# Two down projections with 25 paired steps of seven products instead of 12 paired steps in one of them

## The reference

```python
def conv_ffn(h, w_up, conv_w, conv_b, w_down):
    u = causal_depthwise_conv(h @ w_up, conv_w, conv_b)
    val, gate = jnp.split(u, 2, axis=-1)
    return (jax.nn.gelu(gate) * val) @ w_down      # (256 x 5632) @ (5632 x 2048)
...
for layer in range(DEPTH):                          # DEPTH = 2
    ...
    x = x + conv_ffn(rms_norm(x, ffn_norm[layer]), ...)
```

## Time and profile before

| | us |
|---|---|
| median of three runs | 2266.3 (2266.22 to 2268.31) |
| the profiled execution | 2266.04 |
| its span, first to last instruction | 2264.4 |
| PE busy | 2254.7 |
| DVE busy | 1559.0 |
| ACT busy | 1289.7 |
| POOL busy | 642.8 |
| down0, first to last matmul of layer 0's down projection, about | 967.5 to 1206.8 |
| down1, the same of layer 1's, about | 2028.3 to 2260.8 |

### The profile page before, as it was taken

How to read it: one execution, slowest core, us unless ns; L and a number is a source line. 1 busy time by engine, 2 the same in 40 slices (tenths; PEclk the granted TensorE clock), 3 DMA queues, 4 the chain that set the end, 5 groups by cost and what they waited for, 6 DMA issues and landing times.

```text
span 2264.4 us, 33777 instructions
## 1 busy us (share of the span) xinstructions
PE 2254.7 (100%) x11036; PEld 1902.6 (84%) x11036; DVE 1559.0 (69%) x1892; ACT 1289.7 (57%) x1692; POOL 642.8 (28%) x1051
## 2 busy tenths in 40 slices
PE   9999999999999999999999999999999999999999
PEld 7888888988888888888888888898888888888887
DVE  6766775676767667665556678758767667678666
ACT  6655664565556555554444777556656556555444
POOL 1720001234343343412221000215344343432100
PEclk9999999999999999999999999999999999999999
DMA  8656335546676776766665555646876676778876
GB/s 277 207 197 205 134 123 177 177 152 220 217 224 210 225 218 215 223 208 201 202 204 186 186 186 169 203 140 204 250 223 214 220 222 214 221 226 237 271 225 198
DMA packets 150694, 464.70 MB, mean 205 GB/s; under 512 B 26656, under 2 KB 27552, under 8 KB 150608
## 3 DMA queue, kind: packets, MB, share of 16 engines
q1 hardware_dynamic: 121152, 423.55, 57.1%
q0 software_dynamic: 29312, 39.95, 6.5%
q10 hardware_dynamic: 144, 0.06, 0.0%
HBM read 433.17 MB, written 2.10 MB: 192 GB/s over the span
## 4 chain that ended last, share of the span: by engine, by line
PE 96%; DVE 2%; ACT 1%; issue 1%; DMA 1%; POOL 0%; SPq 0%; ACTq 0%; DVEq 0%
PE ps L475 47%; PE ps L480 23%; PE ps L433 10%; PE ps L437 5%; PE ps L418 2%; PE ps L454 2%; PE ps L1003 2%; PE ps L1005 1%; PE ps L816 1%; PE ps L1108 1%; PE ps L802 0%; DVE w_lo L407 0%; PE ps L896 0%; POOL u_t L2343 0%; DMA u_t<-z_t 0%
## 5 line engine op out<-in xcount | busy, mean ns | idle before, releaser
L379 DVE TENSOR_TENSOR w_lo<-raw,w_hi 128x1024 fp32r<-128x1024 f32 x704 | 875.8, 1247 | 585.2 <-ACT w_hi L373 582.6
L373 ACT ACTIVATE w_hi<-raw 128x1024 fp32r<-128x1024 f32 x703 | 741.6, 1059 | 719.3 <-PE ps L480 599.0
L475 PE MATMUL ps<-w_hi,xg_hl 128*128 128x512 f32 (+1 forms) x3392 | 832.1, 387 | 2.1 <-DVE xg_hl L1604 2.1
L475 PEld LDWEIGHTS ps<-w_hi,xg_hl 128*128 128x128 f32 x3392 | 631.3, 188 | 131.3 <-DVE xg_hl L1604 2.0
L480 PE MATMUL ps<-w_lo,xg_hl 128*128 128x512 f32 (+1 forms) x1696 | 449.4, 387 | 0.0
L480 PEld LDWEIGHTS ps<-w_lo,xg_hl 128*128 128x128 f32 x1696 | 316.4, 188 | 65.3 <-DVE w_lo L379 0.4
L475 PE MATMUL ps<-w_hi,a_hl 128*128 128x512 f32 x1464 | 364.5, 391 | 0.3 <-ACT kmem_tok L1240 0.2
L2343 POOL DMA_DIRECT2D u_t<-z_t x704 | 347.6, 502 | 2.8 <-issue 2.8
L475 PEld LDWEIGHTS ps<-w_hi,a_hl 128*128 128x128 f32 x1464 | 272.8, 188 | 57.5 <-issue 0.7
L480 PE MATMUL ps<-w_lo,a_hl 128*128 128x512 f32 x732 | 195.8, 389 | 0.0
L433 PE MATMUL ps<-xg_hl,w_hi 128*128 128x512 f32 x512 | 161.7, 397 | 0.0
(11 more groups left out here) (247 smaller groups left out, 2101.1 us busy)
## 6 DMA issues: line engine op xcount, KB each, us to landing
raw<-in_w_stream SPq DMA_DIRECT2D x775, 512.0 KB, 4.1
u_t<-z_t POOLq DMA_DIRECT2D x704, 34.0 KB, 3.4
t_in<-in_w_stream SPq DMA_DIRECT2D x24, 256.0 KB, 3.4
t_in<-in_w_stream POOLq DMA_DIRECT2D x24, 256.0 KB, 7.5
raw<-in_w_stream SPq DMA_DIRECT2D x14, 256.0 KB, 4.9
bias<-in_rel_bias POOLq DMA_DIRECT2D x4, 768.0 KB, 6.2
memT<-in_mem_t POOLq DMA_DIRECT2D x4, 512.0 KB, 6.2
gate_w<-in_gate_w POOLq DMA_DIRECT2D x4, 512.0 KB, 3.9
```

The lines of the kernel that those rows point to most:

```text
L373: nc.scalar.activation(w_hi[:, s, :], raw[:, s, :], ACT.Copy).then_inc(hi_done, 1)
L379: nc.vector.tensor_tensor(w_lo[:, s, :], raw[:, s, :], w_hi[:, s, :].bitcast(F), ALU.subtract).then_inc(lo_done, 1)
L475: nc.tensor.matmul(ps[:, bank + tt, 0:n], a[:, k0 + k, tt * P:tt * P + P], w_hi[:, s, k * n:k * n + n], start=start and k == 0 and q == 0, ...
```

## The change

All four pairs of blocks, two in each layer, are now taken with paired steps, and one table, `PAIR_ORDER`, gives their order. In it "a" and "b" are single ordinary units of the first and of the second block of a pair. The numbers of paired steps are 5, 5, 7 and 8 (25), all of the kind "s", for which `ADDING` is 2: two weight sums by DVE, two by adding transfers. (The code also knows a kind "d" with one adding transfer; the table doesn't use it.) In the second pair of layer 0 and in both pairs of layer 1 most steps have one "c" (two units) between them. The activation sums are made in batches at new places (`FORMS_AT`), their splits three and four units later. `t_raw` has one buffer instead of two. In layer 0 DVE, not ACT, puts each block together from the banks (`pair_sums`, `first_block`, `second_block`, `last_parts`), and the last block's two parts are added after the last matmul. The 11 second-block units "b" of layer 0 stand at the end of down0; the turned tiles of three blocks are made ready there.

```diff
-PAIRED = 6
-LAST_ORDER = [...]
-FORMS_AT = [0, 2, 10]
+PAIR_ORDER = \
+    [[("c", u) for u in range(5, 11)] + [x for j in range(4) for x in (("s", j), ("c", 11 + 2 * j), ("c", 12 + 2 * j))]
+     + [("s", 4), ("c", 19), ("c", 20), ("c", 21)],
+     [("a", u) for u in range(5, 16)] + [("c", 16)] + [x for j in range(5) for x in (("s", j), ("c", 17 + j))]
+     + [("b", u) for u in range(5, 16)],
...
+FORMS_AT = [[0, 2, 14], [0, 2, 14, 38]]
...
+        t_raw = [at("t_raw0", XG + size([LAYER_FORMS[0], 4, 2, P]), [UE]), at("t_raw1", ZT, [UE])]
...
+            def down_units(l, c0, c1, steps):
+                for c in range(c0, c1):
+                    old = c - SLOTS
...
+                    sp.wait_ge(lo_done, SPLIT_OF.get(old, old + (EXTRA if l else 0)) + 1)
+                    for n in steps:
+                        if old in (RAW_OF[n], RAW_OF[n] + 1):
+                            sp.wait_ge(wsum_ready, 2 * n + 2)
+                        if c == RAW_OF[n] + 6 and n + 2 in steps:
+                            sums_first(n + 2, l)
...
             def down_section():
-                for n in range(4):
-                    if n < 2:
-                        pe.wait_ge(proj_free, fblock["down0"] + n + 1)
-                    else:
-                        pe.wait_ge(dn_out, TT * (n - 1))
-                    for u in range(TOK_DOWN):
-                        token_unit(...)
+                pe.wait_ge(proj_free, fblock["down0"] + 2)
+                block_pair(0, value_there)
+                block_pair(1, None, lambda tile: pe.wait_ge(dn_out, tile + 1))
...
-            def down_tiles(n):                      # ACT
-                act.wait_ge(pe_unit, first["down0"] + TOK_DOWN * (n + 1))
...
-                for tt in range(TT):
-                    A(y_up[:, tt, :], ps[:, 2 * (n % 2) + tt, :], ACT.Copy).then_inc(dn_out, 1)
...
             def rec_section():                      # DVE
                 c0 = first["rec"]
+                dve.wait_ge(pe_unit, c0)
+                for tt in range(TT):
+                    dve.wait_ge(part_ready, tt + 1)
+                    V.tensor_tensor(y_up[:, tt, :], y_part[:, tt, :], ps[:, 2 + tt, :], ALU.add).then_inc(dn_out, 1)
                 for u in range(U_FULL):
...
+            def down_section():                     # POOL
+                for n in range(2):
+                    added(n)
...
+                move(0)
+                added(PAIRS[0] + 1)
+                move(1)
+                squares(0)
+                for n in range(PAIRS[0] + 2, LAYER_PAIRS[0]):
+                    added(n)
```

More of the change, by code:

```diff
@@ L292, in trunk @@
                         ("rec", N_REC), ("out1", N_OUT), ("xq1", N_XQ), ("xo1", N_XO), ("up1", N_UP), ("down1", N_DOWN)):
[L293 removed]
+            first[name] = c + (EXTRA if name in AFTER else 0)
             assert c % SLOTS == 0
@@ L296, in trunk @@
         N_UNITS = c
[L298 to L304, removed]
-                else:
-                    SPLITS += [("w", c), ("h", c + 1), ("t", n, 0), ("t", n, 1)]
+        GROUPS, SPLIT, RAW_OF, WSUM_SPLIT, SPLIT_OF, SUM_BEFORE, ADDING = [], {}, {}, {}, {}, {}, []
@@ new lines, in trunk @@
+        GROUP_FROM, HALF = [], set()
+        n = 0
+        for g, order in enumerate(PAIR_ORDER):
+            if g % 2 == 0:
+                e = first["down1" if g else "down0"]
+                c = e - (EXTRA if g else 0)
+            GROUP_FROM.append(e)
+            steps = []
+            for kind, u in order:
+                steps.append((kind, u, e, n))
+                parts = [("w", c)] if kind in "ab" else [("w", c), ("w", c + 1)]
+                if kind in "sd":
+                    parts = [("w", c), ("h", c + 1), ("t", n, 0), ("t", n, 1)]
@@ new lines, in trunk @@
+                c += 1 if kind in "ab" else 2
+                e += len(parts)
+            GROUPS.append(steps)
+            if g == 1:
+                assert e == first["rec"]
+        assert c == N_UNITS
+        END = e
+        PAIR_END = GROUP_FROM[1]
+        STEP0 = [sum(PAIRS[:g]) for g in range(len(PAIRS))]
+        LAST_STEP = [STEP0[g] + PAIRS[g] - 1 for g in range(len(PAIRS))]
+        LAST_SPLIT = [WSUM_SPLIT[n, 1] for n in LAST_STEP]
+        FIRST_OF = [[[u for kind, u, _, _ in steps if kind in ("c", "ab"[b])][0] for b in range(2)] for steps in GROUPS]
@@ new lines, in trunk, with adds_until, thirds_until @@
+        LAST_OF = [[max(e + b * (kind == "c") for kind, u, e, _ in steps if kind in ("c", "ab"[b])) for b in range(2)] for steps in GROUPS]
+        def adds_until(n):
+            return 16 * sum(ADDING[m] for m in range(n % 2, n + 1, 2))
+        def thirds_until(n):
+            return ADDING[:n + 1].count(1)
+        ADDS_AT = {LAST_OF[2 + q][b] + SLOTS: (2 * q + b, LAST_OF[2 + q][b]) for q in range(2) for b in range(2)}
+        SUMS_FROM = [max(e for e, x in ADDS_AT.items() if x[0] == 1) + 1, LAST_SPLIT[3] + SLOTS]
@@ L369, in split_hi @@
             s = c % SLOTS
-            act.wait_ge(raw_full[s], times(16 * (c // SLOTS + 1), i, 16 * (per // SLOTS)))
+            before = EXTRA if c >= first["rec"] else 0
+            act.wait_ge(raw_full[s], times(16 * ((c - before) // SLOTS + 1), i, 16 * (per // SLOTS)))
             if c >= SLOTS:
@@ new lines, in block_pair @@
+            def block_pair(g, value_there=None, freed=None):
+                for kind, u, e, n in GROUPS[g]:
+                    if kind in "sd":
+                        paired(g, u, e, n)
+                        continue
+                    for b in (0, 1) if kind == "c" else (0,) if kind == "a" else (1,):
+                        at_unit = e + (b if kind == "c" else 0)
+                        begin, end = u == FIRST_OF[g][b], at_unit == LAST_OF[g][b]
+                        if g == 3 and b and end:
+                            continue
+                        token_unit(pe, at_unit, 2 * u, 2, a_hi, a_lo, 2 * b, begin, end, value_there if b == 0 else None,
+                                   (lambda tt, b=b: freed(2 * b + tt)) if freed and begin else None)
@@ L990, in last_section @@
             def last_section():
-                c0 = first["down1"]
                 def value_there(k):
```

405 lines of the change are left out of this document (239 added, 166 removed).

## The result

The changed kernel takes 2270.95 us as the median of 20 runs (2265.71 to 2279.66), the kernel before 2267.6 us on the same chip (20 runs, 2265.98 to 2274.78). The ratio is 1.0016, 95% interval 1.001 to 1.0023: 0.16% slower, within what was called no change. The forecast was 2259.2 us, with 2256.2 to 2266.5 as its range. So the time is outside the range, and the expected gain of some 7 us became a loss of 3.

What follows compares the result with a forecast made beforehand. PE was taken as the bound, busy 2254.7 of 2264.4 us. 2266.04 - 8.84 - 0.97 + 1.2 + 1.5 = 2258.9, and 0.3 for the median gave 2259.2 us, range 2256.2 to 2266.5.

Steps and rivals of the forecast that it cites:

- The matmul term: Paired steps in both layers: 39 fewer matmuls at 0.2267 us each on PE, 8.84 us won, nothing hiding it.
- The first paired step of down1: PE's waits there for ACT and DVE vanish, with 12 units ahead instead of 10: 0.97 us won.
- The joint: Between down0 and the recurrent block: PE waits before the transposes for DVE's two late additions, 1.2 us lost.
- The rest of DVE, ACT and POOL: Their other work, mainly in layer 0, stays hidden behind PE, counted 0; about 1 us lateness within slack.
- The transfers of the tight intervals: 16 intervals with one "c" use 96% of DMA time; both buffer loops barely close: 1.5 us lost, bounds 0 and 8.6.
- Rival 1: Adding transfers are the bound, `t_in` late in all tight intervals: 2266.3 us, no change; chance 0.17.
- Rival 2: Queues share engines, so the half unit's landing grows from 5.7 to 8.5 us: slower, 2276 us; chance 0.09.
- The last line of the forecast: Forecast is wrong if PE waits over 4 us in tight stretches, or anywhere in down0 where nothing was counted.

Runs made afterwards that it cites:

- Experiment four: Changed kernel with layer 1's down projection back in the order of the kernel before (6 and 6 paired steps), layer 0 as changed: 2271.26 us, ratio 1.0021.
- experiment one: Changed kernel with DVE's addition of the second turned block in down0 ten units later: 2272.31 us, ratio 1.0024.
- five: Changed kernel with POOL issuing the adding transfers of down0's step 7 (counted from 0) ahead of its squares, nothing else: 2271.93 us, ratio 1.0027.
- six: Changed kernel with both the ten-units-later block addition and POOL's adding transfers ahead of its squares in down0: 2264.28 us, ratio 0.9997.
- experiment three: Changed kernel with one batch of down1's activation sums four places later (FORMS_AT 38 to 42): 2265.08 us, ratio 0.9994.
- experiment nine: Changed kernel with only seven steps of down1 making three weight sums by DVE and one by adding transfer: 2266.02 us, ratio 0.9991.
- seven: Changed kernel with all four edits (later block addition, POOL transfers before squares, joint additions before DVE's last split, later activation batch): 2261.19 us, ratio 0.9975.
- eight: Kernel of experiment seven, plus seven steps of down1 with three weight sums by DVE and one adding transfer: 2258.46 us, ratio 0.9968.
- ten: Kernel of experiment eight, plus two steps of down0's second pair with three DVE sums and one adding transfer: 2260.11 us, ratio 0.9972.
- two: Changed kernel with DVE's two additions to `y_up` at the joint ahead of its last split of down0: 2267.25 us, ratio 0.9997.

## Why the forecast was wrong, step by step

**The matmul term** was right: 39 fewer, steps of 4.76 us wherever they run free.

**The first paired step of down1** was right: it does not wait. The gain was 1.5 us, not 0.97, since the two waits cost more than their length. Experiment four, which takes the longer lead away again, waits 3.2 us there.

**The joint** was right in place and releaser, and too small: 1.8 us for 1.2. DVE does two of the recurrent block's input tiles (1.71 us from 1207.32) between the two splits, where I had its last split start at 1208.14; it starts at 1208.95.

```profile
1207.32 1.71 DVE L1669 SCALAR_TENSOR_TENSOR xg_hl<-xT,gains,xg_hl 128x256 fp32r<-128x256 f32 x2
1208.95 1.21 DVE L427 TENSOR_TENSOR w_lo<-raw,w_hi 128x1024 fp32r<-128x1024 f32 x1
1210.08 1.27 DVE L2336 TENSOR_TENSOR y_up<-y_part,ps 128x512 f32<-128x512 f32 x2
```

**The rest of DVE, ACT and POOL** is the step that failed. I had counted "about 1 us of lateness for the seventh step, within the slack", and in all 0. It is the 7.0 us of down0. I priced what DVE and POOL have to do, and not when `x_add(1)` can start. Its moves take 10.8 us to issue and 4.8 more to land, and the sums and splits behind it on DVE are a paired step's, not a plain unit's. The forecast names POOL's queue but takes the issues as its only load; `squares(0)`, 6.0 us long beside an idle DVE, stands between them and the next adding transfers. Experiments one, five and six show both gates: one late addition moves the wait to the next step (6.95 us), the POOL edit alone makes it 6.1, and only both together free the steps.

**The transfers of the tight intervals**, put at 1.5 us, is the second term that failed, in its size: down1 lost 6.9, still under the bound of 8.6. Two edits, each alone, leave little of it: moving the batch of sums (experiment three, 0.6 us lost), and making fewer adding transfers (nine, 1.5). The same down1 without either lost 3.7 to 6.9 in four profiles, so a part of it is chance. It is not one cause. At the batch a late landing and 2.9 us of DVE work, put between a step's sums and its half split, add up to more than the slack. DVE at 2111 to 2118:

```profile
2111.30 0.69 DVE L2134 TENSOR_TENSOR t_raw<-t_in,raw 128x512 f32<-128x512 f32 x1 [2.00 <-DMA raw<-in_w_stream]
...
2113.77 1.22 DVE L2097 TENSOR_TENSOR s_f<-a_hl 128x1024 f32<-128x1024 f32 x1
...
2116.28 0.42 DVE L2105 TENSOR_TENSOR s_f<-s_f 128x256 f32<-128x256 f32 x1
2116.62 0.69 DVE L457 TENSOR_TENSOR w_lo<-raw,w_hi 128x512 fp32r<-128x512 f32 x1
```

DVE waits 2.00 us for `raw`, then does the batch; the half split that PE wants ends at 2117.3. Ahead of the 1.86 us no batch is in the way. DVE's sums begin late, after a wait for a whole unit that landed 9.3 us after its issue, and the adding transfers issued just ahead of it at 2225.6 and 2226.2 took up to 9.8:

```profile
2236.25 0.69 DVE L2134 TENSOR_TENSOR t_raw<-t_in,raw 128x512 f32<-128x512 f32 x1 [4.84 <-DMA raw<-in_w_stream]
```

What the transfers cost by themselves, once the orders are mended, is the difference of experiments seven and eight on one chip, 2.7 us, near the 1.5 taken. The intervals of the two ratios overlap, so this size is only a rough one.

**Rival 1** (adding transfers are the bound) showed its signs only in part. The median of the adding transfers is 7.2 us, not 9 or more, but single ones take up to 9.8. DVE's sums wait for `t_in` three times in 2060 to 2240, 8.5 us in all, and did not before; they wait more for `raw`, 20.8 us in all, and did so before, 26.7. **Rival 2** is not borne out, though its direction is: the half unit lands in 6.8 us where it took 5.7, and a whole one in 6.1. The half unit's landing goes with the tight order (6.5 to 7.1 us in experiments three, eight, nine and ten) and not with the wide one (5.5 in experiment four). The Trainium skill's page "DMA: Bandwidth & Descriptors", section "Queues, rings and completion order", has each DMA engine go round its queues, by which two queues would slow each other. No run here shows that price by itself: in experiment nine, with six adding transfers fewer and nothing else changed, the half unit takes 7.1 us.

**The clock** was in no term. Of the 15.7 us lost, some 4.5 are not waits but matmuls at the lower level behind the waits of 3.88 and 1.86 us. So the forecast's slope, one us lost per us of wait, was too flat.

The last line of the forecast held: wrong "if PE waits [...] anywhere in down0 where I counted nothing". The step that failed is thus the 0 for "the rest of DVE, ACT and POOL", 7.0 us in place of it; the transfers' term gave 5.4 us more than its 1.5, and the joint 0.6 more.

## What to carry to other kernels

When a step is made dearer for an in-order engine, go through every instruction that stands in the queue ahead of it and ask when that one can start, down to the issue of its last transfer, and do the same on the engine that issues that transfer. When an edit at the obvious culprit gives nothing, look for a second gate behind it before dropping the theory: here two edits were worth nothing or less one by one, and some 4 us together. And a new wait in a PE that had no gap can cost more than its length: here 0.3 us more at the least, and 3.1 us more in the worst case, where the clock fell.

## What the runs showed of the hardware

**The clock can fall behind a short wait, and its length doesn't settle it.** Behind waits of PE of 3.88, 6.95 and 1.86 us the 512-column matmuls start 0.43 us apart instead of 0.23 (for 6.1 us behind the first, for 3.7 behind the last). That is the 1.2 GHz level, 512 / 1.2 = 427 ns. Behind waits of 1.57 and 1.58 us they don't, nor behind the 3.69 us of experiment nine, whose windows show a granted clock of 1.00 throughout. The wait of 3.88 us, at the same place in three profiles, cost 7.0, 5.7 and 5.8 us (changed kernel, experiments three and two). So a time with such a wait in it varies by some us with nothing changed.

**VectorE and GpSimd slow each other.** A squaring of 128x256 on POOL takes 0.61 us while DVE waits (changed kernel, 1126 to 1130) and 1.48 while DVE splits and adds (experiment one, same place); with the POOL edit alone DVE's four block additions take 2.91 us instead of 2.21, and a weight sum 1.20 instead of 0.69. With both edits, and POOL quiet, the four additions take 1.42 us. The Trainium skill's page "SBUF — State Buffer", section "Who interferes with whom", says that a VectorE instruction with two SBUF inputs contends with a GpSimd instruction that reads SBUF; the trace agrees. For this reason an edit that frees DVE of a wait makes POOL slower at once.

**A better kernel.** The 25 steps with the four edits and seven steps of the other kind take 2258.46 us (six runs, 2257.74 to 2259.5) against 2265.89 before on that chip, 0.32% faster. That is within 1 us of the time that the forecast had given the change, but reached by other means: the orders mended and seven adding transfers fewer.
